# A chunked RWKV-7 scan on one Trainium2 core: the triangular inverse kept as 32x32 diagonal blocks instead of full 64x64 matrices

## The chip, the cores and the metric

The kernel runs on one core of one Trainium2 chip. The metric is the device time of one execution in microseconds (us), lower is better. Durations and waits come from one profiled execution of the kernel before.

## What is computed

The reference is a two-layer backbone over 256 latent tokens and 256 context tokens, width 1024. Each layer has three mixers (a bidirectional RWKV-7 scan, latent attention, a Fourier mix), a gated merge and a feed-forward network. The change touches the scan alone:

```python
def rwkv_scan(state0, f, d, reverse):
    ...
    def step(S, inp):
        r_t, w_t, k_t, v_t, kk_t, b_t = inp
        sa = -jnp.einsum("bhvk,bhk->bhv", S, kk_t)
        S = S * w_t[:, :, None, :] + sa[..., None] * b_t[:, :, None, :] + v_t[..., None] * k_t[:, :, None, :]
        return S, jnp.einsum("bhvk,bhk->bhv", S, r_t)
```

It has 8 heads of 64, two directions, and in each layer runs over the context first and then over the latent tokens. All of it is float32.

## The kernel before

**Chunks.** The scan takes 64 tokens at a time. Within a chunk the 64 values of `sa` depend on each other through a strictly triangular 64x64 matrix L, so `sa` comes from the inverse of I + L. Each layer has 512 tokens, which makes 8 chunk steps, and the two layers make 16. A step does both directions (d = 0 and 1) beside each other. Layer 1 needs the outputs y in all 8 steps, layer 2 in the last 4 only, so 12 steps have the work for y and 4 have not.

**Layout.** Two heads lie one above the other on the 128 partitions (`UP` is partitions 0 to 63, `DOWN` is 64 to 127), and four such pairs lie beside each other. `each` (L1250) issues 8 matmuls for one product of all heads: 4 pairs times two, each 64 rows by 64 columns, on the two diagonal 64x64 tiles of TensorE. The profile has two records for each float32 matmul, so `x16` is one such product.

**A step on TensorE (PE), in its order.** (1) For each direction the Gram products (L1281, L1282, L1287): B against Q and R into bank B_LT (128 columns), Q against B into B_L (64 columns), K against Q and R into B_G (128 columns). (2) Transposes of B and K (L1292) and of V (L1301). (3) Levels 1 to 4 of the inverse (L1303 to L1318): the inverse T is built from blocks of 2, 4, 8, 16, 32. POOL masks L into `LM` (L1060), PE multiplies LM by T (`x1`), ACT copies the product to `X1` (L1116), PE multiplies T by X1 and X1 by T (`tx`, two products), and DVE subtracts both from T and its transpose (`T2`, L1208). (4) Level 5 joins the two 32x32 halves: `halves` (L1263) does it with 8 matmuls of 32x32 for each product, and DVE subtracts (L1213). (5) W (L1329), the part of y that comes from the state (L1335), `sa` = T times W (L1341, by `each`), the part of y that comes from `sa` (L1347), and the state product (L1356). Then the next step's Gram products follow.

**What waits for what.** The engines run through semaphores, one queue each, in the order that is written. In a level PE waits for DVE (T) and POOL (LM), ACT and POOL for PE, PE again for ACT (X1), and DVE for PE. DVE has other work between the levels in its queue: `gram_out` (L1183) and `keep` (L1173) after levels 1 and 2, the next chunk's `operands` (L1164 to L1166) and `exponents` (L1152, L1153) after level 3, and `operands` again after level 5. DVE also makes level 0 (L1194 masks, L1196 adds the identity, L1200 masks ARB). ACT copies `WS` (L1133) before `sa` and SA_V (L1137) after it; both parts behind `sa` on PE wait for L1137.

## Time and profile before

| | us |
|---|---|
| median of 3 runs | 2377.68 (2368.16 to 2380.21) |
| the profiled execution, its own time | 2380.61 |
| its span, first to last instruction | 2378.8 |
| PE busy in the span | 2090.7 |
| DVE busy | 1170.2 |
| ACT busy | 832.9 |
| POOL busy | 340.1 |

The two scans lie from about 234.5 to 489.5 us and from 1589.8 to 1837.7 us of the span. A row of the timeline has the start, how long it lasted, the engine, the line, what is written and read, the number of records, and in brackets how long the engine was idle before it and what released it. The times of PE rows include the time until the last result is there. PEclk 1.00 is 2.4 GHz and 0.50 is 1.2 GHz.

### The profile page before, as it was taken

What the parts mean: (1) busy time and instruction counts of PE and PEld (TensorE: products, weight loads), DVE (VectorE), ACT (ScalarE), POOL (GpSimd) and SP (SyncE); (2) the same over time, 40 slices, a digit from 0 to 9 for tenths busy, and PEclk for the clock granted to TensorE, in tenths of its full rate; (3) what the DMA queues carried; (4) which work ended last, traced back from release to release, by engine and by line L of the source; (5) the groups of instructions that cost most, each with busy time, mean ns of one, the idle gap of its engine ahead of it and who ended that gap; (6) DMA issues with size and microseconds to landing.
All of it is one profiled execution on the core that took longest, in us unless ns stands there. A gap on an engine that the chain in (4) does not pass through costs nothing. (4 is left out here: it accounts for less than half of the span.)

```text
span 2378.8 us, 46796 instructions
## 1 busy us (share of the span) xinstructions
PE 2090.7 (88%) x19559; PEld 1651.7 (69%) x19559; DVE 1170.2 (49%) x1849; ACT 832.9 (35%) x1515; POOL 340.1 (14%) x444
## 2 busy tenths in 40 slices
PE   4886889869989999889998997968888798988998
PEld 2562788844457888658886665738887446988988
DVE  1635787762462333353332216477777435545544
ACT  1333443423342222242222113264443244434442
POOL 1102333301100011010001001043332020000000
PEclk7997999989989999989999998979999899998999
DMA  7416000030111333222235753000000311553553
GB/s 261 142 62 230 2 0 2 1 118 21 36 38 54 98 94 101 71 71 94 88 102 218 283 168 124 27 1 1 1 1 26 113 36 56 169 178 124 178 174 128
DMA packets 144521, 219.40 MB, mean 92 GB/s; under 512 B 6846, under 2 KB 123800, under 8 KB 137216
## 3 DMA queue, kind: packets, MB, share of 16 engines
q1 hardware_dynamic: 142880, 215.74, 26.7%
q8 instruction: 101, 1.65, 0.3%
q0 software_dynamic: 1504, 1.71, 0.2%
q14 instruction: 36, 0.29, 0.0%
HBM read 208.00 MB, written 9.44 MB: 91 GB/s over the span
## 5 line engine op out<-in xcount | busy, mean ns | idle before, releaser
L367 PE MATMUL BANK<-H_high,W_high 128*128 128x512 f32 (+2 forms) x1472 | 526.4, 358 | 79.5 <-ACT H_high L628 36.1
L331 DVE TENSOR_TENSOR W_low<-RING,W_high 128x1024 fp32r<-128x1024 f32 x268 | 328.2, 1234 | 459.1 <-ACT W_high L328 459.1
L368 PE MATMUL BANK<-H_low,W_high 128*128 128x512 f32 (+2 forms) x1472 | 520.3, 353 | 0.0
L369 PE MATMUL BANK<-H_high,W_low 128*128 128x512 f32 (+2 forms) x1472 | 519.7, 353 | 0.0
L328 ACT ACTIVATE W_high<-RING 128x1024 fp32r<-128x1024 f32 x268 | 279.3, 1052 | 614.8 <-PE BANK L369 597.9
L367 PEld LDWEIGHTS BANK<-H_high,W_high 128*128 128x128 f32 (+1 forms) x1472 | 283.5, 193 | 134.6 <-issue 52.1
L369 PEld LDWEIGHTS BANK<-H_high,W_low 128*128 128x128 f32 (+1 forms) x1472 | 283.9, 193 | 38.1
L368 PEld LDWEIGHTS BANK<-H_low,W_high 128*128 128x128 f32 (+1 forms) x1472 | 284.2, 193 | 36.6 <-issue 1.1
L1255 PE MATMUL BANK<-RING,WORK 64*64 64x64 f32 x4096 | 166.8, 220 | 17.2 <-DVE RING L1208 8.7
L1255 PEld LDWEIGHTS BANK<-RING,WORK 64*64 64x64 f32 x4096 | 145.4, 134 | 29.9 <-issue 29.5
L1060 POOL TENSOR_TENSOR WORK<-WORK,masks 128x256 f32<-128x256 f32 x160 | 125.3, 795 | 115.6 <-PE BANK L1255 115.0
L367 PE MATMUL BANK<-hidden_high,W_high 128*128 128x512 f32 (+1 forms) x352 | 121.8, 346 | 12.0 <-PEq L2062 12.0
L368 PE MATMUL BANK<-hidden_low,W_high 128*128 128x512 f32 (+1 forms) x352 | 119.5, 339 | 0.0
L369 PE MATMUL BANK<-hidden_high,W_low 128*128 128x512 f32 (+1 forms) x352 | 119.3, 339 | 0.0
L1255 PE MATMUL BANK<-WORK,RING 64*64 64x64 f32 x2560 | 107.8, 224 | 4.1 <-issue 1.8
L1116 ACT ACTIVATE WORK<-BANK 128x256 f32<-128x256 f32 (+1 forms) x160 | 56.5, 362 | 133.4 <-PE BANK L1255 124.5
L2000 POOL TENSOR_TENSOR merge_tiles<-merge_tiles 128x512 f32<-128x512 f32 (+1 forms) x32 | 33.8, 1067 | 480.2 <-DVE merge_tiles L1982 480.2
L1255 PEld LDWEIGHTS BANK<-WORK,RING 64*64 64x64 f32 x2560 | 93.4, 139 | 9.4 <-issue 7.7
L1208 DVE TENSOR_TENSOR RING<-RING,BANK 128x512 f32<-128x512 f32 x128 | 83.8, 683 | 31.6 <-PE BANK L1255 29.0
L1255 PE MATMUL BANK<-RING 64*64 64x128 f32 (+1 forms) x1536 | 78.3, 261 | 21.1 <-DVE RING L1166 21.1
L367 PEld LDWEIGHTS BANK<-hidden_high,W_high 128*128 128x128 f32 x352 | 67.3, 191 | 34.9 <-issue 27.7
L1255 PEld LDWEIGHTS BANK<-RING 64*64 64x64 f32 x1536 | 74.5, 139 | 23.2 <-issue 22.3
(281 smaller groups left out, 3110.9 us busy)
## 6 DMA issues: line engine op xcount, KB each, us to landing
modulation_weights<-w_mod_dram SPq DMA_DIRECT2D x48, 1024.0 KB, 6.9
RING<-w_in_dram SPq DMA_DIRECT2D x46, 1024.0 KB, 5.9
RING<-w_ffn_in_dram SPq DMA_DIRECT2D x44, 1024.0 KB, 5.1
RING<-w_ffn_out_dram SPq DMA_DIRECT2D x20, 1024.0 KB, 5.1
RING<-w_out_dram SPq DMA_DIRECT2D x8, 1024.0 KB, 5.4
h_high<-H_high SPq DMA_DIRECT2D x2, 2048.0 KB, 8.2
h_low<-H_low SPq DMA_DIRECT2D x2, 2048.0 KB, 12.5
H_high<-h_high SPq DMA_DIRECT2D x2, 2048.0 KB, 12.0
```

The lines of the kernel that those rows point to most:

```text
L328: high_ready.mark(nc.scalar.activation(self.part(0, c), self.raw(c), ACT.Copy))
L331: low_ready.mark(nc.vector.tensor_tensor(self.part(1, c), self.raw(c), self.part(0, c).bitcast(FP32), ALU.subtract))
L367: nc.tensor.matmul(out, w[0], x[0], start=start, stop=False)
L368: nc.tensor.matmul(out, w[0], x[1], start=False, stop=False)
L369: return nc.tensor.matmul(out, w[1], x[0], start=False, stop=stop)
L1060: s_lm[d].mark(nc.gpsimd.tensor_tensor(LM[d], LTS[d], lanes(level_mask(d, l)), ALU.mult))
L1116: s_x1_out[d].mark(nc.scalar.activation(X1[d][:, :, cols], pairs(4 * d + B_L, 0)[:, :, cols], ACT.Copy))
L1208: s_t[d].mark(nc.vector.tensor_tensor(T2[d].rearrange("p q j t -> p (q j t)"), T2[d].rearrange("p q j t -> p (q j t)"), BANK[:, 4 * d + B_ ...
L1255: last = nc.tensor.matmul(BANK[rows, bank, at + j * stride:at + j * stride + width], lhs(j)[rows], rhs(j)[rows], start=True, stop=True)
L2000: pool_sig.mark(nc.gpsimd.tensor_tensor(total(m), total(m), gate(u), ALU.add))
```

## The change

T2 now holds three sets of 32x32 blocks: the diagonal blocks of T, those of its transpose, and the one off-diagonal block. Levels 1 to 4 need only the diagonal blocks. `each_block` takes the place of `each` there: 16 matmuls of 32 rows by 32 columns in place of 8 of 64 by 64, on the four diagonal tiles in turn. The tiles that DVE, ACT and POOL handle in the levels become half as wide.

```diff
-    T2 = [scratch(2, PAIRS, HD) for _ in range(NDIR)]
+    T2 = [scratch(3, PAIRS, BLOCK) for _ in range(NDIR)]
...
-    LTS = [scratch(PAIRS, HD) for _ in range(NDIR)]
-    LM = [scratch(PAIRS, HD) for _ in range(NDIR)]
-    X1 = [scratch(PAIRS, HD) for _ in range(NDIR)]
+    LTS = [scratch(2, PAIRS, BLOCK) for _ in range(NDIR)]
+    LM = [scratch(PAIRS, BLOCK) for _ in range(NDIR)]
+    X1 = [scratch(PAIRS, BLOCK) for _ in range(NDIR)]
```

TensorE: the Gram products that feed the inverse are made block by block (`gram_blocks`, 64 rows by 32 columns), the levels by `each_block`, level 5 by `across` (as many matmuls as `halves`), and `sa` by two matmuls for each head, one with the diagonal block (32 rows) and one with the two blocks of the other row (64 rows):

```diff
+                def each_block(bank, at, lhs, rhs):
+
+                    for j in range(PAIRS):
+                        for b in range(P // BLOCK):
+                            rows = slice(b * BLOCK, (b + 1) * BLOCK)
+                            last = nc.tensor.matmul(BANK[rows, bank, at + j * BLOCK:at + (j + 1) * BLOCK], lhs[rows, j], rhs[rows, j],
+                                                    start=True, stop=True)
+                    return last
...
+                def gram_blocks(bank, at, lhs, rhs, wide=None):
+
+                    for j in range(PAIRS):
+                        for half in (slice(0, BLOCK), slice(BLOCK, HD)):
+                            for h, rows in enumerate((UP, DOWN)):
+                                if half == wide:
+                                    out = BANK[of_head(h, half), bank, HALF:2 * HALF].rearrange("p (b j t) -> p b j t", b=2, j=PAIRS)[:, :, j]
+                                    cols = slice(0, HD)
+                                else:
+                                    out, cols = BANK[of_head(h, half), bank, at + j * BLOCK:at + (j + 1) * BLOCK], half
+                                last = nc.tensor.matmul(out, lhs(j)[rows, half], rhs(j)[rows, cols], start=True, stop=True)
...
-                        s_gram[d].mark(each(bank + B_LT, 0, 2 * HD, lambda j: BK[d][:, j, 0], qr))
-                        s_gram[d].mark(each(bank + B_L, 0, HD, q, lambda j: BK[d][:, j, 0], 2 * HD))
+                        gram_blocks(bank + B_LT, near(d), b, q, wide=first_half(d))
+                        s_gram[d].mark(each(bank + B_LT, 0, HD, b, lambda j: QR[d][:, j, 1]))
+                        s_gram[d].mark(gram_blocks(bank + B_L, near(d), q, b))
...
-                                s_x1[d].mark(each(4 * d + B_L, 0, HD, lambda j: LM[d][:, j], lambda j: T2[d][:, 0, j]))
+                                s_x1[d].mark(each_block(4 * d + B_L, 0, LM[d], T2[d][:, 0]))
...
-                                each(4 * d + B_LT, 0, HD, lambda j: T2[d][:, 1, j], lambda j: X1[d][:, j])
-                                s_tx[d].mark(each(4 * d + B_LT, HALF, HD, lambda j: X1[d][:, j], lambda j: T2[d][:, 1, j]))
+                                each_block(4 * d + B_LT, 0, T2[d][:, 1], X1[d])
+                                s_tx[d].mark(each_block(4 * d + B_LT, BLOCKS, X1[d], T2[d][:, 1]))
...
-                        s_sa[d].mark(each(4 * d + B_LT, 0, HD, lambda j: T2[d][:, 1, j], lambda j: WS[d][:, j]))
+                        for j in range(PAIRS):
+                            for h, rows in enumerate((UP, DOWN)):
+                                one = of_head(h, first_half(d))
+                                out = slice(j * HD, (j + 1) * HD)
+                                nc.tensor.matmul(BANK[one, 4 * d + B_LT, out], T2[d][one, 1, j], WS[d][one, j], start=True, stop=True)
+                                last = nc.tensor.matmul(BANK[of_head(h, later_half(d)), 4 * d + B_LT, out], T2[d][rows, 2, j], WS[d][rows, j],
+                                                        start=True, stop=True)
+                        s_sa[d].mark(last)
```

The other engines: ACT gets one more pair of copies for each direction in level 5 and a new signal `s_later` that `sa` waits for, POOL no longer masks in level 5, and DVE writes the off-diagonal block with a copy in place of the subtraction.

```diff
-                        for d in range(NDIR):
+                        for d in range(NDIR if l < NL else 0):
...
-                            s_x1_out[d].mark(nc.scalar.activation(X1[d][:, :, cols], pairs(4 * d + B_L, 0)[:, :, cols], ACT.Copy))
+
+                            s_x1_out[d].mark(nc.scalar.activation(X1[d], blocks(4 * d + B_L, 0), ACT.Copy, scale=1.0 if l < NL else -1.0))
+                        for d in range(NDIR if l == NL else 0):
+
+                            act.wait_ge(*at_step(s_t[d], i, LEVELS, NL))
+                            act.wait_ge(*at_step(s_sa[d], i))
+                            for h in range(2):
+                                rows = of_head(h, later_half(d))
+                                last = nc.scalar.activation(T2[d][rows, 2], T2[d][rows, 1], ACT.Copy)
+                            s_later[d].mark(last)
...
-                                    last = nc.vector.tensor_tensor(T2[d][rows, 1, :, cols], T2[d][rows, 1, :, cols],
-                                                                   pairs(4 * d + B_LT, HALF)[rows, :, cols], ALU.subtract)
+                                    rows = of_head(h, first_half(d))
+                                    last = nc.vector.tensor_copy(T2[d][rows, 2], blocks(4 * d + B_LT, BLOCKS)[rows])
```

TensorE's queue at the end of a step, before. The names in these rows are those of whole memories; the last numbers are the output's partitions by its columns. L1268 is level 5, L1329 is W, L1335 the first part of y, L1255 is `sa`, L1347 the second part of y, L1356 the state product.

```order
L1268 MATMUL BANK<-RING,WORK 32x32 x32
L1329 MATMUL BANK<-WORK,RING 64x64 x16
L1335 MATMUL BANK<-RING,WORK 64x64 x16
L1339 REGISTER_ALU
L1255 MATMUL BANK<-WORK,RING 64x64 x16
L1347 MATMUL BANK<-WORK 64x64 x16
L1356 MATMUL BANK<-WORK 64x64 x16
```

The same place now. L1296 is level 5, L1373 W, L1379 the first part of y, L1390 and L1391 are `sa`; they alternate 16 times (6 of the 32 rows are shown).

```order
L1296 MATMUL BANK<-RING,WORK 32x32 x16
L1373 MATMUL BANK<-WORK,RING 64x64 x16
L1379 MATMUL BANK<-RING,WORK 64x64 x16
L1383 REGISTER_ALU
L1390 MATMUL BANK<-WORK,RING 32x64
L1391 MATMUL BANK<-WORK,RING 32x64
L1390 MATMUL BANK<-WORK,RING 32x64
L1391 MATMUL BANK<-WORK,RING 32x64
L1390 MATMUL BANK<-WORK,RING 32x64
L1391 MATMUL BANK<-WORK,RING 32x64
```

The one group of 16 matmuls of a single form became 32 matmuls, and their form changes from each one to the next.

TensorE's queue at the start of a step (the Gram products), before:

```order
L1255 MATMUL BANK<-RING 64x128 x8
L1255 MATMUL BANK<-RING 64x64 x8
L1255 MATMUL BANK<-RING 64x128 x16
L1255 MATMUL BANK<-RING 64x64 x8
L1255 MATMUL BANK<-RING 64x128 x8
L1292 MATMUL BANK<-ident,RING 128x128 x8
```

The same place now, from the end of the first direction's first product on:

```order
L1310 MATMUL BANK<-RING 32x32 x2
L1274 MATMUL BANK<-RING 64x64 x8
L1310 MATMUL BANK<-RING 32x32 x16
L1274 MATMUL BANK<-RING 64x128 x8
L1310 MATMUL BANK<-RING 32x32 x2
L1310 MATMUL BANK<-RING 32x2x32 x2
```

Each direction had 24 matmuls of one form. It now has 48, with three changes between the forms of L1310 and L1274 within it and one more to the next direction.

## Rows read from the trace of the kernel before

**Rows 1.** The page, busy time of each engine over the whole span.

```profile
PE 2090.7 (88%) x19559; PEld 1651.7 (69%) x19559; DVE 1170.2 (49%) x1849; ACT 832.9 (35%) x1515; POOL 340.1 (14%) x444
```

**Rows 2.** Busy time by stretch: stretch, its length, then each engine.

```profile
core 0: us, PE busy (x) PEld busy (x) DVE busy (x) ACT busy (x) POOL busy (x), PEclk, DMA share, GB/s
234.50:489.50 255.00, 225.86 (x5746) 207.82 (x5742) 189.75 (x328) 107.38 (x278) 91.73 (x127) 0.98 0.01 1
1589.80:1837.70 247.90, 219.27 (x5486) 201.88 (x5482) 186.72 (x320) 107.24 (x278) 91.97 (x127) 0.97 0.00 1
```

**Rows 3.** Timeline of POOL, the first row of three successive steps.

```profile
1742.00 0.18 POOL L1052 COPY decay_kept<-decay 64x8 f32<-64x8 f32 x1 [8.53 <-DVE WORK L1239]
...
1774.73 0.18 POOL L1052 COPY decay_kept<-decay 64x8 f32<-64x8 f32 x1 [10.01 <-DVE WORK L1239]
...
1805.91 0.18 POOL L1052 COPY decay_kept<-decay 64x8 f32<-64x8 f32 x1 [8.47 <-DVE WORK L1239]
```

**Rows 4.** Timeline of PE in the step from 1774 us on.

```profile
1773.82 4.64 PE L1255 MATMUL BANK<-RING 64*64 64x128 f32 x96
...
1781.49 0.68 PE L1255 MATMUL BANK<-RING,WORK 64*64 64x64 f32 x16 [0.42 <-DVE RING L1196]
...
1789.81 0.66 PE L1255 MATMUL BANK<-RING,WORK 64*64 64x64 f32 x16
1790.28 0.66 PE L1255 MATMUL BANK<-WORK,RING 64*64 64x64 f32 x16
...
1797.46 0.61 PE L1268 MATMUL BANK<-RING,WORK 32*32 32x32 f32 x32 [0.66 <-ACT WORK L1116]
1798.00 1.15 PE L1329 MATMUL BANK<-WORK,RING 128*64 128x64 f32 x32
1798.98 1.10 PE L1335 MATMUL BANK<-RING,WORK 128*64 128x64 f32 x32
1800.02 1.15 PE L1255 MATMUL BANK<-WORK,RING 64*64 64x64 f32 x32
1801.66 1.47 PE L1347 MATMUL BANK<-WORK 64*64 64x64 f32 x32 [0.49 <-ACT WORK L1137]
1803.07 2.08 PE L1356 MATMUL BANK<-WORK 128*64 128x64 f32 x32
```

**Rows 5.** Timeline of DVE, levels 1 to 4 of the same step.

```profile
1783.24 0.69 DVE L1208 TENSOR_TENSOR RING<-RING,BANK 128x512 f32<-128x512 f32 x1 [1.13 <-PE BANK L1255]
1784.08 0.69 DVE L1208 TENSOR_TENSOR RING<-RING,BANK 128x512 f32<-128x512 f32 x1
...
1787.15 1.28 DVE L1208 TENSOR_TENSOR RING<-RING,BANK 128x512 f32<-128x512 f32 x2
...
1791.00 1.29 DVE L1208 TENSOR_TENSOR RING<-RING,BANK 128x512 f32<-128x512 f32 x2
1792.20 0.42 DVE L1164 TENSOR_TENSOR RING<-WORK 128x256 f32<-128x256 f32 x1
1792.54 0.42 DVE L1165 TENSOR_TENSOR RING<-WORK 128x256 f32<-128x256 f32 x1
...
1794.95 1.27 DVE L1208 TENSOR_TENSOR RING<-RING,BANK 128x512 f32<-128x512 f32 x2
```

**Rows 6.** Groups with their forms: mean duration of one record in ns.

```profile
L1255 PE MATMUL BANK<-RING,WORK 64*64 64x64 f32 x4096 | 166.8, 220 | 17.2 <-DVE RING L1208 8.7 <-DVE RING L1196 4.9 <-issue 1.1
L1268 PE MATMUL BANK<-RING,WORK 32*32 32x32 f32 x1024 | 25.0, 193 | 19.2 <-DVE RING L1208 9.0 <-ACT WORK L1116 9.0
L1116 ACT ACTIVATE WORK<-BANK 128x256 f32<-128x256 f32 x128 | 49.0, 383 | 128.0 <-PE BANK L1255 124.5
L1116 ACT ACTIVATE WORK<-BANK 128x128 f32<-128x128 f32 x32 | 7.5, 275 | 5.4 <-PE BANK L1268 5.1
```

**Rows 7.** Timeline of ACT between level 5 and W.

```profile
1797.51 0.59 ACT L1130 ACTIVATE WORK<-BANK 64x512 f32<-64x512 f32 x1
1798.73 0.85 ACT L1133 ACTIVATE WORK<-BANK 128x256 f32<-128x256 f32 x2 [0.63 <-PE BANK L1329]
```

**Rows 8.** Busy time by stretch, around two falls of the clock (columns as in Rows 2).

```profile
1762.60:1765.90 3.30, 2.04 (x84) 1.87 (x86) 1.45 (x4) 2.69 (x9) 0.72 (x1) 1.00 0.00 0
1766.00:1769.30 3.30, 3.30 (x66) 3.18 (x62) 1.58 (x5) 0.77 (x2) 0.00 (x0) 0.50 0.00 0
...
1670.50:1673.80 3.30, 1.97 (x87) 1.70 (x83) 1.65 (x4) 2.73 (x9) 0.72 (x1) 1.00 0.00 0
1673.90:1677.20 3.30, 3.30 (x63) 3.12 (x59) 2.23 (x7) 1.05 (x4) 0.00 (x0) 0.50 0.00 0
```

More of the change, by code:

```diff
@@ L65 @@
 LEVELS = 6
+BLOCK = 32
 SLOTS = 3
@@ L125, in shape_constants @@
         level = []
-        for l in range(LEVELS):
+        for l in range(LEVELS - 1):
             b = 1 << l
@@ L133, in shape_constants @@
         parts = [-(level[0].T.astype(f)), -(level[0].astype(f))] + [m.astype(f) for m in level[1:]]
-        parts += [strict_t.astype(f), incl_t.astype(f)]
-        masks.append(np.concatenate([stack(m) for m in parts], axis=1))
+        block_masks += [np.concatenate([m[0:BLOCK, 0:BLOCK]] * (P // BLOCK), axis=0) for m in parts]
+        masks += [stack(strict_t.astype(f)), stack(incl_t.astype(f))]
     out["masks"] = np.concatenate(masks, axis=1).astype(f)
-    out["eye_heads"] = stack(np.eye(HD)).astype(f)
+    out["block_masks"] = np.concatenate(block_masks, axis=1).astype(f)
+    out["eye_blocks"] = np.concatenate([np.eye(BLOCK)] * (P // BLOCK), axis=0).astype(f)
     return out
@@ L981, in build_in @@
     NL = LEVELS - 1
+    NM = NL - 1
     N = SEG_CHUNKS
     def lanes(mask):
-        return mask.unsqueeze(1).to_broadcast([P, PAIRS, HD])
+        return mask.unsqueeze(1).to_broadcast([P, PAIRS, BLOCK])
     STEPS = 2 * N
@@ L1032, in scan @@
         pairs = lambda bank, a: BANK[:, bank, a:a + HALF].rearrange("p (j t) -> p j t", j=PAIRS)
+        BLOCKS = PAIRS * BLOCK
+        blocks = lambda bank, a: BANK[:, bank, a:a + BLOCKS].rearrange("p (j t) -> p j t", j=PAIRS)
+        near = lambda d: HALF + BLOCKS * d
         with stage() as block:
@@ L1239, in step @@
                         s_st[d].mark(nc.vector.tensor_tensor(STATE_V[d][UP], STATE_V[d][UP], SD[d][UP], ALU.add))
+                for d in range(NDIR):
+                    nc.vector.memset(BANK[:, 4 * d + B_LT, HALF:2 * HALF], 0.0)
                 nc.vector.memset(STATE_V[0][UP], 0.0)
@@ L1267, in halves @@
                             k = of_head(h, k_rows)
-                            last = nc.tensor.matmul(BANK[of_head(h, out_rows), bank, at + j * HD + out_cols.start:at + j * HD + out_cols.stop],
-                                                    lhs[k, j, out_rows], rhs[k, j, out_cols], start=True, stop=True)
+                            last = nc.tensor.matmul(BANK[of_head(h, out_rows), bank, at + j * BLOCK:at + (j + 1) * BLOCK], lhs[k, j], rhs[k, j],
+                                                    start=True, stop=True)
+                    return last
+                def gram_blocks(bank, at, lhs, rhs, wide=None):
[8 more added lines that the diff above has]
+                                last = nc.tensor.matmul(out, lhs(j)[rows, half], rhs(j)[rows, cols], start=True, stop=True)
                     return last
```

58 lines of the change are left out of this document (32 added, 26 removed).

## The prediction

> **What bounds the kernel now.** I read the busy shares first. Over the whole span PE is busy 2090.7 of 2378.8 us [rows 1], but a busy PE is not a PE at its peak, and the change touches the two scans alone. Busy time by stretch gives them 255.0 and 247.9 us, 503 us together or 21% of the span, and in both PE (89%) and DVE (75%) are busy side by side [rows 2]. So neither has much slack there. Everything else keeps its instructions, and I cost it at nothing: the new constants are one small load more behind loads that nobody in the opening waits for.
>
> POOL's first row of a step gives the pitch of the steps: 1774.73 to 1805.91, 31.2 us, and 32.7 us for the step before it [rows 3]. There are 16 steps, so 0.1 us in a step is 1.6 us of the kernel. The timeline of PE shows what a step is made of [rows 4], that of DVE who sets the pace of the levels [rows 5]: in level 1 DVE waits 1.13 us for PE, but the pairs of L1208 at 1787.15, 1791.00 and 1794.95 begin with no wait, right behind DVE's other work. In levels 2 to 4 DVE is the bound, with the round trip PE, ACT, PE close behind it.
>
> **What the change gains.** One product of a level is 16 records on two tiles, and the next begins 0.47 us after it (1789.81 to 1790.28) [rows 4]. The new product has 32 records of 32x32. The nearest row is L1268, which has 32 such records in 0.61 us [rows 4], of which 0.19 is the latency of the last [rows 6]: 0.42 us. It uses two tiles for each direction and the new product uses four at once, so 0.42 is the upper end that I use, and half of it, 0.21, the lower. I take 0.35: a gain of 0.1 us a product. The Trainium skill ("TensorE: Matmul & The Clock Gate", section "Measured speedup vs the span model") has tiles of a pack start about 4 ns apart; by it the product would be at the lower end, and the sum below some 1.5 us a step lower.
>
> The pair of L1208 works on 512 columns a direction in 1.28 us. With 256 columns the nearest rows are L1164 and L1165: 0.42 us for one and the next 0.34 us behind it, so 0.76 for a pair [rows 5]. That is 0.5 us less in each of levels 2 to 4, all of it on the path there: 1.5 us. In level 1, where PE is waited for, three products of a direction, a copy on ACT (383 to 275 ns [rows 6]) and the subtraction shrink, about 0.3 + 0.1 + 0.2 = 0.6 us. At the start of the levels L1194 and L1196 become half as wide, and PE's wait of 0.42 us for L1196 [rows 4] goes. Level 5 has as many matmuls as before. POOL's mask halves and is off the path. Together **2.5 us a step gained**. The bounds: 1.5 if the new products take as long as the old ones, 4.0 if they take 0.21.
>
> **What it costs.** The main term is a cost on PE that the old order pays only a few times a step. When the form of the matmuls (rows by columns of the tile) changes, the next one starts late. L1347 (64x64) lasts 1.47 from 1801.66; less the 0.22 of its last record, that record starts at 1802.91, and L1356 (128x64) starts at 1803.07: 0.16 us. From L1268 (32x32, last start 1797.46 + 0.61 - 0.19 = 1797.88) to L1329 (128x64) at 1798.00 it is 0.12. Between two products of one form it is 1789.81 + 0.66 - 0.22 = 1790.25 to 1790.28: 0.03 [rows 4, 6]. So a change costs 0.12 to 0.16 us from start to start, about 0.1 more than none.
>
> *sa.* It was 16 matmuls of one form, 1.15 us less 0.22, 0.93 us [rows 4]. It is now 32 matmuls that alternate between a 32x32 tile (L1390) and a 64x32 tile (L1391), 32 changes. Each matmul is two records on one tile; their distance is about 0.05 us (16 records of 64x64 on two tiles in 0.47 us are 0.058 apart on one tile, with somewhat wider weights [rows 4]). 0.05 + 0.13 = 0.18 us a matmul, 5.8 us in place of 0.93: **4.9 us a step**. The lower bound is 0.15 (3.9 us), the upper 0.22 (6.1 us). It lies on the path: y and the state product are queued behind it on PE, L1137 on ACT waits for it, and the next step's Gram products follow. One piece comes back: PE waited 0.49 us for L1137 [rows 4], and the first direction's L1137 is now hidden behind the second direction's `sa`. I take back 0.4: 4.5 us.
>
> *Gram products.* The 96 records were 4.64 us [rows 4]. There are now 8 changes of form in them at 0.1, 0.8 us, and the narrower streams give back some 0.4 (the 128-column product of L becomes blocks of 64 and 32 columns). Cost **0.4 us**, between 0 and 1.
>
> *ACT.* Four copies of 32x128, at most 0.28 each by the 128x128 copy [rows 6], come between L1116 and L1130. ACT was idle 0.63 us before L1133 [rows 7], and `sa` began 0.44 us after L1133 was done (1799.58 to 1800.02). These two cover the 0.8 to 1.1 us, so nothing; if that cover is gone (the 4 steps without y), up to 0.4 us each, under 2 us in all.
>
> Without the clock, a step costs 4.5 + 0.4 - 2.5 = 2.4 us more, 16 steps 38 us.
>
> **The clock.** In the scans PE's granted clock is 0.98 and 0.97 on the mean [rows 2]. It falls to 0.50 (1.2 GHz) now and then, each time behind the stretch with level 5, where PE had run 32x32 matmuls with waits between them: 1762.6 to 1765.9 had PE busy 2.04 of 3.30 us, and 1766.0 to 1769.3 ran at 0.50; 1670.5 to 1673.8 and 1673.9 to 1677.2 are the same [rows 8]. The step with the first of these falls is the one that took 32.7 us in place of 31.2 [rows 3]: 1.5 us a fall. After the change all the levels run on 32x32 matmuls, and `sa` is 5.8 us in which the array mostly waits. I expect two more such stretches in each step: **3.0 us a step**, 48 us in all. Nothing excludes none, nor four.
>
> **The sum.** 2380.6 (the profiled execution) + 38 + 48 = 2467 us. That execution lies 3 us above the median of the runs, so the forecast is **2464 us**, slower by 3.6%.
>
> **The rivals.**
> 1. *The forms' changes cost what I say and the clock holds.* For it: after `sa` the Gram products are as dense as before. Against it: [rows 8]. 2377.7 + 38 = 2416 us.
> 2. *Faster.* The place is `sa`: if PE does not wait between a 32x32 and a 64x32 matmul, it is 32 matmuls of 0.05 us spread over tiles, about 1 us as now, and the clock then falls about as rarely as now. 2.5 - 0.4 = 2.1 us a step gained, 34 us: 2344 us. It decides where a change costs less than 0.1 - 2.4/32 = about 0.03 us. For it: the trace of before has no such pair of forms. Against it: both kinds of change above, one of rows alone and one of rows and columns, cost 0.12 us or more from start to start. The Trainium skill ("TensorEngine Tiling (Array Packing)", section "Key Properties") says that each change of the tiling mode drains the engine, which leaves this rival little.
> 3. *The levels themselves get slower.* If a 32x32 record cannot come faster than a 64x64 one does, 0.029 us, a product of 32 records takes 0.93 us in place of 0.47. That is 24 products by 0.47, 11 us a step; about two thirds of it show, since PE then bounds the levels: 7 us more and the gain of 1.0 on PE gone, 2464 + 16 x 8 = 2590 us. Against it: L1268 has its 32 records in 0.42 us, 0.013 each. The Trainium skill ("TensorEngine Tiling (Array Packing)", section "Instruction Overhead") has about 60 cycles for each matmul however few its columns are, and warns against cutting a dimension that is small already; that speaks against this change, and the row speaks against the rule.
>
> **How the numbers follow.** My forecast has a chance of 0.55 (its own range 2416 to 2530: the bounds of `sa`, of the levels and of one to four stretches of low clock), rival 1 has 0.25, rival 2 has 0.12, rival 3 has 0.05, and 0.03 is left for no real difference (gain and cost cancel). About 0.5% is what a measurement of this kernel can tell from no change. The range that leaves out rival 2 and rival 3 and keeps the low side of rival 1 is 2380 to 2535. Slower by over 0.5% are my forecast, rival 1 and rival 3, 0.85 together, less 0.02 for the low end of rival 1: 0.83. Faster by over 0.5% is rival 2: 0.12. The same is what is left: 0.05.
>
> **What would show it.** Right: in the timeline L1390 and L1391 as alternating rows about 0.18 us apart, some 5.8 us from the first to the last; L1227 (the old L1208) at about 0.42 us; the products of L1287 at most 0.42 us apart; a mean clock in the scans of 0.7 to 0.9. Wrong: `sa` under 2 us; products of L1287 over 0.5 us apart; a clock that stays at 0.97; or a step shorter than 31 us.

## The result and the profile after

The changed kernel takes **2740.5 us** (median of 4 runs, 2739.19 to 2745.27) against 2376.3 for the kernel before beside it: ratio 1.1538, 95% interval 1.152 to 1.1556. It is slower, as forecast, but by 364 us and not by 86, and above the range. All of it lies in the two scans. In the profiled execution (span 2738.9 us, mean clock 0.835, before 0.943) they end near 670 and 2200 us, where they ended at 489.5 and 1837.7 [rows 2].

Of the page, the busy time of PE, the fetches of program code (queue q8), and the groups of the levels with their idle time, as in [rows 1] and [rows 6]:

```profile
PE 2323.6 (85%) x27751; PEld 1784.7 (65%) x27751; DVE 1093.5 (40%) x1853; ACT 840.2 (31%) x1579; POOL 274.7 (10%) x412
...
q8 instruction: 242, 3.96, 0.6%
...
L1287 PE MATMUL BANK<-RING,WORK 32*32 32x32 f32 x8192 | 158.8, 224 | 93.7 <-issue 90.5
...
L1227 DVE TENSOR_TENSOR RING<-RING,BANK 128x256 f32<-128x256 f32 x128 | 53.9, 421 | 223.6 <-PE BANK L1287 223.2
...
L1287 PE MATMUL BANK<-WORK,RING 32*32 32x32 f32 x4096 | 85.5, 225 | 48.5 <-issue 43.5
```

DVE's merge is as short as forecast (421 ns), and DVE now waits for PE. But PE's products of the levels have 134 us of idle time ahead of them that ends on nothing but "issue", where the old products had 2.9 (L1255, groups of 4096 and 2560). And q8 fetched 242 pieces of code; the page of before has 101. The lines of before, beside the one in [rows 6]:

```profile
q8 instruction: 101, 1.65, 0.3%
...
L1255 PE MATMUL BANK<-WORK,RING 64*64 64x64 f32 x2560 | 107.8, 224 | 4.1 <-issue 1.8
```

Busy time by stretch, as in [rows 2]: the clock in the scans is 0.62 and 0.61, not 0.98 and 0.97.

```profile
234.50:670.00 435.50, 339.97 (x9693) 272.46 (x9684) 151.37 (x328) 109.84 (x308) 56.27 (x105) 0.62 0.02 4
1760.00:2200.00 440.00, 340.83 (x9615) 267.53 (x9608) 154.48 (x339) 112.41 (x313) 60.56 (x112) 0.61 0.03 7
```

POOL's first row of three steps, as in [rows 3]: 54.8 and 58.6 us, in place of 31 to 33.

```profile
1968.81 0.18 POOL L1061 COPY decay_kept<-decay 64x8 f32<-64x8 f32 x1 [20.51 <-DVE WORK L1256]
...
2023.58 0.18 POOL L1061 COPY decay_kept<-decay 64x8 f32<-64x8 f32 x1 [24.22 <-DVE WORK L1256]
...
2082.16 0.18 POOL L1061 COPY decay_kept<-decay 64x8 f32<-64x8 f32 x1 [24.22 <-DVE WORK L1256]
```

The timeline of PE in the levels of the step behind the third of these rows shows both sides of the change, as in [rows 4]:

```profile
2095.72 0.75 PE L1287 MATMUL BANK<-RING,WORK 32*32 32x32 f32 x64
2096.67 0.42 PE L1287 MATMUL BANK<-WORK,RING 32*32 32x32 f32 x29 [0.20 <-ACT WORK L1126]
...
2096.95 0.40 PE L1287 MATMUL BANK<-RING,WORK 32*32 32x32 f32 x23
2099.51 0.26 PE L1287 MATMUL BANK<-RING,WORK 32*32 32x32 f32 x8 [2.16 <-issue]
...
2099.93 1.70 PE L1287 MATMUL BANK<-RING,WORK 32*32 32x32 f32 x84
2103.19 0.42 PE L1287 MATMUL BANK<-RING,WORK 32*32 32x32 f32 x11 [1.56 <-issue]
...
2104.72 0.54 PE L1287 MATMUL BANK<-RING,WORK 32*32 32x32 f32 x20
2107.34 0.43 PE L1287 MATMUL BANK<-RING,WORK 32*32 32x32 f32 x12 [2.08 <-issue]
```

A product of 32 records begins 0.28 us behind the start of the one before it (2096.67 to 2096.95), so records come 0.009 us apart. Then, in the middle of a product, PE stands for 2.16 us. The pauses end 3.7 and 4.2 us apart, and between them lie about 128 records, 64 matmuls. The pause of 2.16 us lies where the granted clock is 1.00 (2094 to 2100 us), so a lowered clock is not its cause. The DMA view of one step points at the reason: 12 pieces of code in 58.6 us, of 0.20 MB / 12 = 16 KB each. In the same view of two steps of before (1742 to 1806 us), no packet is moved.

```profile
GB/s 0 11 0 0 11 0 0 0 11 0 0 11 0 0 11 0 0 11 0 11 0 0 11 0 0 11 0 0 11 0 0 0 0 0 0 0 0 0 11 11
DMA packets 12, 0.20 MB, mean 3 GB/s; under 512 B 0, under 2 KB 0, under 8 KB 0
...
q8 instruction: 12, 0.20, 1.4%
```

The same view of 2096 to 2108 us, in slices of 0.3 us, has its three pieces at 2097, 2100.6 and 2104.5 us. Each is fetched some 2.4 to 2.8 us before a pause ends, and the next only some 1.3 us after PE has begun again. So the distance of 3.7 to 4.2 us is that of about 64 matmuls and the way of one piece. Whether pieces could come closer together if they were asked for sooner, no run shows.

The second part of the loss is `sa`. Its alternating rows are 0.35 us apart and not 0.18, and the whole takes 2065.26 to 2076.35, 11.1 us. The row by stretch over it says where a part of this comes from: granted clock 0.50, 1.2 GHz.

```profile
2065.26 0.42 PE L1390 MATMUL BANK<-WORK,RING 32*32 32x64 f32 x2
2065.60 0.42 PE L1391 MATMUL BANK<-WORK,RING 64*32 64x64 f32 x2
2065.95 0.41 PE L1390 MATMUL BANK<-WORK,RING 32*32 32x64 f32 x2
...
2076.35 2.14 PE L1399 MATMUL BANK<-WORK 64*64 64x64 f32 x32
...
2065.26:2076.70 11.44, 11.44 (x72) 5.97 (x72) 0.00 (x0) 1.00 (x3) 0.00 (x0) 0.50 0.01 1
```

### The profile page after: what moved, and what is told of

Same layout as the page of the kernel before. It is cut to its first block and busy times, and to the rows that moved or that the text cites. A ratio compares the mean times of both kernels' runs of the same rounds, so it can differ in the third digit from the quotient of the medians.

```text
span 2738.9 us, 63339 instructions
## 1 busy us (share of the span) xinstructions
PE 2323.6 (85%) x27751; PEld 1784.7 (65%) x27751; DVE 1093.5 (40%) x1853; ACT 840.2 (31%) x1579; POOL 274.7 (10%) x412
## 5 line engine op out<-in xcount | busy, mean ns | idle before, releaser
L1287 PE MATMUL BANK<-RING,WORK 32*32 32x32 f32 x8192 | 158.8, 224 | 93.7 <-issue 90.5
L1287 PEld LDWEIGHTS BANK<-RING,WORK 32*32 32x32 f32 x8192 | 133.0, 136 | 105.0 <-issue 103.4
L1227 DVE TENSOR_TENSOR RING<-RING,BANK 128x256 f32<-128x256 f32 x128 | 53.9, 421 | 223.6 <-PE BANK L1287 223.2
L1126 ACT ACTIVATE WORK<-BANK 128x128 f32<-128x128 f32 x160 | 44.3, 277 | 276.4 <-PE BANK L1287 226.3
L1287 PE MATMUL BANK<-WORK,RING 32*32 32x32 f32 x4096 | 85.5, 225 | 48.5 <-issue 43.5
L1287 PEld LDWEIGHTS BANK<-WORK,RING 32*32 32x32 f32 x4096 | 70.0, 137 | 64.3 <-issue 63.0
L1391 PE MATMUL BANK<-WORK,RING 64*32 64x64 f32 x512 | 101.2, 296 | 0.0
L1390 PE MATMUL BANK<-WORK,RING 32*32 32x64 f32 x512 | 99.9, 292 | 0.0
L1310 PE MATMUL BANK<-RING 64*32 64x32 f32 (+1 forms) x2048 | 46.4, 230 | 43.6 <-issue 22.5
```

The lines of the kernel that those rows point to most:

```text
L1126: s_x1_out[d].mark(nc.scalar.activation(X1[d], blocks(4 * d + B_L, 0), ACT.Copy, scale=1.0 if l < NL else -1.0))
L1227: s_t[d].mark(nc.vector.tensor_tensor(both, both, BANK[:, 4 * d + B_LT, 0:HALF], ALU.subtract))
L1287: last = nc.tensor.matmul(BANK[rows, bank, at + j * BLOCK:at + (j + 1) * BLOCK], lhs[rows, j], rhs[rows, j], start=True, stop=True)
L1310: last = nc.tensor.matmul(out, lhs(j)[rows, half], rhs(j)[rows, cols], start=True, stop=True)
L1390: nc.tensor.matmul(BANK[one, 4 * d + B_LT, out], T2[d][one, 1, j], WS[d][one, j], start=True, stop=True)
L1391: last = nc.tensor.matmul(BANK[of_head(h, later_half(d)), 4 * d + B_LT, out], T2[d][rows, 2, j], WS[d][rows, j], start=True, stop=True)
```

## The experiments

My theory after the result: the 364 us are (a) code that no longer stays loaded in PE, with pauses wherever the small matmuls run densely, (b) the order of forms in `sa`, and (c) a clock that falls behind both. The rivals: the pauses belong to the small matmuls themselves, or to the clock, or to the jump back of the loop.

Most of the kernels below ran once. The runs of the kernel before lie between 2368 and 2380 us, so a difference of under some 12 us between two single runs is not shown by these alone.

**sa_grouped.** The 32x32 matmuls of `sa` of a direction first, then the 64x32 ones: 4 changes of form a step instead of 32.

```diff
                         for j in range(PAIRS):
-                            for h, rows in enumerate((UP, DOWN)):
+                            for h in range(2):
...
                                 nc.tensor.matmul(BANK[one, 4 * d + B_LT, out], T2[d][one, 1, j], WS[d][one, j], start=True, stop=True)
+                        for j in range(PAIRS):
+                            for h, rows in enumerate((UP, DOWN)):
+                                out = slice(j * HD, (j + 1) * HD)
                                 last = nc.tensor.matmul(BANK[of_head(h, later_half(d)), 4 * d + B_LT, out], T2[d][rows, 2, j], WS[d][rows, j],
                                                         start=True, stop=True)
```

> The changed kernel with the 16 matmuls of sa in each direction sorted by form: 8 of 32x32, then 8 of 64x32, so 4 changes of form a step in place of 32. Theory (each change of form waits until the array is empty, and sa's 11.1 us a step are that): sa falls to about 2 to 3 us, the kernel by 16 x 8.5 = 136 us or more, to about 2600. Rival (the new forms themselves are slow, 0.35 us a matmul whatever stands beside them): no difference, 2740.

Measured 2618.6 us, 122 less. Order alone is worth a third of the loss. The steps are still 41.5 to 51.3 us, and the pauses are still there: PE has 135.4 us of idle time on "issue" ahead of the products of the levels.

**before_unrolled.** The kernel before, with the loop over steps written out on every engine.

```diff
-                Signal.trips = end - first
-                with eng.Fori(first, end) as i:
+                Signal.trips = 1
+                for i in range(first, end):
```

> The kernel before with the scan's loops written out, so that no code is used twice; the work is the same. Theory (the pauses of about 2 us on TensorE in the changed kernel come from 16 KB pieces of code that are fetched at a rate that only dense short matmuls outrun): code is fetched in all steps, about 6 pieces a step, and the time stays within 1% of before, with at most a few pauses. Rival (each fetch of code costs a pause of 2 us wherever it is): 14 steps x 6 x 2 = 168 us slower, about 2545.

Measured 2380.3 us, no difference. This execution fetched 157 pieces, 12 of them from 1742 to 1806 us, and its clock in the first scan is 0.98. The two groups of L1255 have 3.6 us of idle time on "issue", as little as before. So fetching code is not a cost in itself: a step of before spends 64 matmuls in 31.2 x 64 / 368 = 5.4 us, more than the 3.7 to 4.2 us between two pieces in the changed kernel.

**y_interleaved and y_in_turn.** The kernel before with 28 more changes of form (64x64 and 128x64) in each step with y, and its control with the same matmuls in turn.

```diff
                         order = [(k, one) for one in heads() for k in range(2)]
+                        order = [x for x in order if x[0] == 0] + [x for x in order if x[0] == 1]
```

(The line with + stands in y_in_turn alone.)

> As y_in_turn, but with the 8 matmuls of y (64x64) and the 8 of the state product (128x64) of a direction in turn: 31 changes of form in a step with y in place of 3, the number of matmuls unchanged. Theory (a change costs 0.12 to 0.16 us from start to start at 2.4 GHz, up to 0.24 at 1.2 GHz): 28 x 0.1 to 0.2 x 12 steps = 34 to 67 us over y_in_turn, about 2425. Rival (a change of form between other forms is free, and only 32-row against 64-row tiles wait): no difference from y_in_turn.

> The kernel before with the second part of y and the state product of one direction behind each other, then the other direction; in a step with y that is 3 changes of form in place of 1. It is the control for y_interleaved. Both theories: within 1% of before, perhaps 0.5% slower (2 changes x 0.12 us x 12 steps = 3 us).

Measured 2481.5 and 2379.2 us: 102 us for 12 x 28 = 336 changes, 0.30 us each with the clock. I had expected 34 to 67 us: the mechanism held, and my price for a change was too low by half or more. The timeline of y_interleaved has a matmul of two records each 0.25 us at the full clock and each 0.40 us at half:

```profile
1844.19 0.33 PE L1355 MATMUL BANK<-WORK 128*64 128x64 f32 x2
1844.45 0.32 PE L1350 MATMUL BANK<-WORK 64*64 64x64 f32 x2
1844.70 0.33 PE L1355 MATMUL BANK<-WORK 128*64 128x64 f32 x2
...
1810.13 0.47 PE L1350 MATMUL BANK<-WORK 64*64 64x64 f32 x2
1810.54 0.47 PE L1355 MATMUL BANK<-WORK 128*64 128x64 f32 x2
```

So a pair of forms with no 32-row tile in it costs this too, and the rival that only 32-row against 64-row tiles wait is out.

**levels_looped.** PE's levels 1 to 4 as a loop of four turns inside the step: the same matmuls run, but PE's body has 336 matmuls in the code and not 624. The transposes of V of direction 1 move behind level 4, and ACT's copy of them to level 5.

```diff
+                    turn_values(0)
+                    if True:
+                        Signal.trips *= NL - 1
+                        with pe.Fori(1, NL) as l:
+                            level(l)
+                        Signal.trips //= NL - 1
...
+                    turn_values(1)
+                    level(NL, True)
```

> The changed kernel with TensorE's levels 1 to 4 of a step as a loop of its own of four turns, so that its products stand once in the code and not four times: the same matmuls run, TensorE's loop body shrinks from about 2,500 instructions (624 matmuls of 4) to about 1,350 (336). The transposes of the values of direction 1 move behind level 4. Theory (the pauses of 1.5 to 2.2 us on no wait, some 12 us a step, are TensorE waiting for its own code, because the body no longer stays loaded): the code fetches inside the loop and the pauses go, 16 steps x 12 us = 190 us less: 2,550 us. Rival 1 (the pauses belong to the small matmuls or to the lowered clock, not to code): they stay, 2,740 us. Rival 2 (each jump back costs a pause of about 2 us as the one behind the step's own jump, 4 more a step): 2,550 + 16 x 8 = 2,680 us, with the pauses at the levels' ends instead of inside the groups.

**levels_written_out.** The control: the same placement, with `for l in range(1, NL)` in place of the loop.

> The control for levels_looped: the same placement of the transposes of the values of direction 1 behind level 4, with the levels written out as in the changed kernel, so that TensorE's loop body has about 2,500 instructions again. Theory (code): the pauses are back, 2,720 to 2,760 us. Rival (moving the transposes gave part of the 219 us): below 2,700 us.

Measured **2521.3 us** with the loop and **2761.6 us** without: 240 us by nothing but how often the code stands in the program. q8 has 97 pieces in place of 242, and the steps are 38 to 39 us, but for the first turn of each loop (42 to 45 us). Of the page of levels_looped, the larger group of the levels: its idle time was 93.7 us, 90.5 of it on "issue", and DVE ends most of what is left.

```profile
L1287 PE MATMUL BANK<-RING,WORK 32*32 32x32 f32 x8192 | 120.6, 202 | 34.7 <-DVE RING L1227 24.3
```

The rival that the small matmuls pause by themselves is out, and so is a pause for every jump back. The control is 21 us slower than the changed kernel: with the transposes moved, the idle time on "issue" ahead of the products of the levels is 154.6 us in place of 134.

**levels_looped_grouped.** Both edits.

> As levels_looped, and with the sa product's 32 matmuls ordered by form (8 of 32x32, then 8 of 64x32, for each direction). If code and changes of form are separate costs, the 122 us that ordering alone gave come off as well: 2,550 - 122 = 2,430 us. If what ordering gave was mostly fewer pauses or a clock that follows from them, less comes off: 2,500 us or more. A time below 2,376 us would mean that the idea of the change was sound and only its code order was not.

Measured 2393.4 us: 128 less, as much as ordering gave with the pauses there. The two costs add. The steps are now 30 to 31 us, but the first turn of each loop takes 35 to 36. PE's timeline of such a turn, and the busy time by stretch around it:

```profile
1719.62 0.86 PE L1287 MATMUL BANK<-RING,WORK 32*32 32x32 f32 x64
...
1724.12 0.28 PE L1287 MATMUL BANK<-WORK,RING 32*32 32x32 f32 x10 [2.52 <-issue]
...
1712.00:1722.00 10.00, 9.11 (x362) 7.72 (x360) 6.16 (x12) 4.15 (x9) 4.38 (x8) 1.00 0.02 5
1722.00:1732.00 10.00, 6.62 (x427) 6.07 (x427) 6.45 (x13) 2.35 (x9) 2.54 (x5) 0.68 0.01 2
```

One pause for code of 2.5 us, and the clock falls behind it: this is how (a) can bring (c). No run takes the clock by itself.

**after_short and before_short.** Levels 2 to 4 with one pair of heads in four, in the changed kernel and in the one before.

```diff
-                    for j in range(PAIRS):
+                    for j in range(n):
...
-                                s_x1[d].mark(each_block(4 * d + B_L, 0, LM[d], T2[d][:, 0]))
+                                s_x1[d].mark(each_block(4 * d + B_L, 0, LM[d], T2[d][:, 0], PAIRS if l < 2 else 1))
...
```

> The changed kernel with levels 2, 3 and 4 of the inverse left out for three of the four pairs of heads (the result is not the inverse then; 216 of 624 matmuls a step go), in straight code: the loop body has about 1,700 instructions without any inner loop. Theory (code): no fetches inside the loop and no pauses on no wait over 1 us; steps of 30 to 36 us, 2,390 us. Rival (the pauses come from dense small matmuls): pauses of 2 us stay in level 1 and beside it, at least 4 us a step, and the steps are 40 us, 2,500 us.

> The control for after_short: the kernel before, with levels 2, 3 and 4 left out for three of the four pairs in the same way (108 of 368 matmuls a step). Its levels are bounded by the chain through four engines, so that little goes: steps of 27 to 29 us against 31, 2,310 to 2,350 us. What after_short is above it is the price of the sa product's and the Gram products' changes of form, with the clock, without code pauses: 32 changes x 0.25 to 0.35 us a step as a bound would be 8 to 11 us x 16 = 130 to 180 us; less what the levels gain.

Measured 2579.6 and 2397.3 us; both expectations missed. A body of 408 matmuls (some 1,690 instructions) was not short enough everywhere. The two loops of the first scan have the same body, and yet one fetched 8 or 9 pieces in every turn and the other none. Busy time by stretch of a turn of the first and one of the second, and the DMA view of the first:

```profile
320.60:368.00 47.40, 37.59 (x800) 29.34 (x800) 18.80 (x42) 13.97 (x40) 7.53 (x14) 0.64 0.01 3
459.10:500.00 40.90, 34.80 (x803) 26.57 (x802) 18.66 (x43) 14.04 (x40) 7.53 (x14) 0.67 0.00 0
```

```profile
q8 instruction: 9, 0.15, 1.3%
```

The same 800 records take 47.4 us with fetches and 40.9 without. So the steps of 30 to 36 us that I expected were not reached without fetches either: the rest of the miss is the order of `sa` and the clock, 0.67 in that turn. Why the one loop kept its code and the other did not (where it lies in the program is what differs) was not tried.

before_short does less than the kernel before and is 19 us slower (one run). Its clock is what differs: 0.79 in the first scan, where the full kernel has 0.98 [rows 2].

```profile
234.50:489.50 255.00, 196.48 (x3836) 174.03 (x3833) 183.31 (x320) 104.49 (x271) 88.18 (x122) 0.79 0.00 1
```

PE has less to do between the waits for the same chain, and the clock falls more often. That the one brings the other is my reading.

**after_unrolled.** The changed kernel with the loops over steps written out: no jump back.

> The changed kernel with its two loops of a scan written out on every engine: 8 steps in a row, no jump back, every piece of code is used once. If the pauses come from the rate at which pieces of code arrive (one for 64 matmuls), they stay and the time is that of the changed kernel within 1%: 2,720 to 2,770 us. If they come from the jump back, which throws loaded code away, they go: 2,560 us or less.

Measured 2693.3 us, 47 less than with the loops and below what I expected of the rate alone. In the changed kernel the first product behind a jump back (L1310) has 22.5 us of idle time on "issue"; here that is gone, so the jump back has a part, some 47 us with what follows from it. But most of the cost of code stays when every piece is used once. The groups of the levels have 130 us on "issue", as against 134:

```profile
L1287 PE MATMUL BANK<-RING,WORK 32*32 32x32 f32 x8192 | 155.9, 225 | 90.3 <-issue 85.8
...
L1287 PE MATMUL BANK<-WORK,RING 32*32 32x32 f32 x4096 | 85.5, 226 | 49.0 <-issue 44.3
```

**gram_one_loop.** levels_looped_grouped with the 64x32 products of a direction ahead of its 64x64 ones, and the first scan in one loop of 7 steps.

```diff
+                        s_gram[d].mark(gram_blocks(bank + B_L, near(d), q, b))
                         gram_blocks(bank + B_LT, near(d), b, q, wide=first_half(d))
                         s_gram[d].mark(each(bank + B_LT, 0, HD, b, lambda j: QR[d][:, j, 1]))
-                        s_gram[d].mark(gram_blocks(bank + B_L, near(d), q, b))
```

> levels_looped_grouped, and two more edits of order: of the Gram products of each direction the 64x32 ones (L and its transpose) come first and the 64x64 ones behind, which takes 2 changes of form for a direction and 4 for a step away; and the first scan, whose two halves have the same step, runs as one loop of 7 steps, so that its first turn's extra time (35.5 against 30 us, a code pause of 2.5 us and the lowered clock behind it) is paid once, not twice. 4 x 0.145 us x 16 = 9 us and 5 us: 2393 - 14 = 2,379 us. If Gram is hidden behind another engine: 2,388 us.

Measured 2384.6 us, 9 less, which two single runs do not show by themselves. The timelines do: from the first Gram product to the transposes behind them it is 5.18 us in levels_looped_grouped (1778.04 to 1783.22) and 4.68 with the new order (side_work_spread, 1793.45 to 1798.13), both at a clock of 1.00. That is 0.5 us a step, 8 us in all: a small term.

**split_merge.** DVE's merge as two operations, the first behind the first product.

```diff
-                                s_t[d].mark(nc.vector.tensor_tensor(both, both, BANK[:, 4 * d + B_LT, 0:HALF], ALU.subtract))
+                                s_ta[d].mark(nc.vector.tensor_tensor(one[0], one[0], BANK[:, 4 * d + B_L, BLOCKS:2 * BLOCKS], ALU.subtract))
+                                dve.wait_ge(*at_step(s_tx[d], i, NL, l))
+                                s_t[d].mark(nc.vector.tensor_tensor(one[1], one[1], BANK[:, 4 * d + B_LT, BLOCKS:2 * BLOCKS], ALU.subtract))
...
```

> gram_one_loop, and VectorE's merge of T and its transpose in levels 1 to 4 as two operations of half the columns instead of one, the first of which starts behind the first of the two products (which goes to another bank for that). The next level's first product needs T alone. If the wait of 0.68 us on VectorE's merge ahead of each level's first product is what bounds a level, it shrinks by the second product (0.21 us) and by half of the merge (0.42 to 0.25 us), about 0.4 us x 4 levels x 16 steps = 25 us: 2,355 us, below the kernel before. Rival (the wait moves on to the merge of the transpose, or to ScalarE's copy): 2,380 us as gram_one_loop.

**side_work_spread and spread_split_merge.** DVE's masking of the Gram products of direction 1 goes behind level 4, both copies of q and r behind level 2; the second also has the split merge.

```diff
-                        if l <= NDIR:
-                            gram_out(l - 1)
-                            keep(i, l - 1)
+                        if l in (1, 4):
+                            gram_out(l // 4)
+                        if l == 2:
+                            keep(i, 0)
+                            keep(i, 1)
```

> gram_one_loop (2,384.6 us), with VectorE's work between the merges placed otherwise: the masking of the Gram products of direction 1 behind level 4 instead of level 2, the copies of q and r of direction 0 behind level 2 instead of level 1. In split_merge VectorE's merge started only when 2.4 us of such work behind levels 1 and 2 was done. If that holds the levels here too: up to 0.3 us x 2 levels x 16 = 10 us less: 2,375 us. If a level is bound by the chain x1, copy, products, merge: 2,385 us.

> side_work_spread with the merge split in two (as in split_merge, 2,379.6 us). With VectorE free when the first product is done, a level ends 0.3 to 0.4 us sooner: 4 levels x 0.35 x 16 = 22 us: 2,355 us. If the levels are bound by the chain through ScalarE's copy and the wait before the second products: 2,375 us.

Measured 2379.6, 2373.7 and 2385.7 us. Spreading DVE's work came out 11 us lower, but the steady steps with y are alike (30.8 us in gram_one_loop, 30.7 here), so it is not shown that the spreading did it. Splitting the merge came out 5 lower without it and 12 higher with it, no more than single runs differ. None of the 22 to 25 us that I expected of it came: that the wait for the merge bounds a level to the amount I took was wrong.

**before_looped.** The control: the kernel before with PE's level loop, the one loop in the first scan and DVE's side work spread in the same way.

> The kernel before with the edits of form that the better variants of the changed kernel have: TensorE's levels 1 to 4 as a loop of four turns, one loop of 7 steps in the first scan, VectorE's side work at other levels (as in side_work_spread). Its code stayed loaded anyway and its levels are bounded by VectorE's merges of 1.1 us, so that nothing is to be gained but the first turns' 1.8 us: 2,365 to 2,385 us. Should it be much faster, the forms' gain is not the change's.

**before_looped_timed and side_work_spread_timed.** Both again, in turns with the kernel before.

> before_looped again, timed in turns with the kernel before: one look gave 2,362.96 against 2,375.79 us. If the edits of form alone make the kernel before faster, the ratio is 0.993 to 0.997 with an interval below 1; if one look misled, it holds 1.

> side_work_spread again, timed in turns with the kernel before: one look gave 2,373.68 against 2,375.79 us: ratio 0.997 to 1.001. Against before_looped_timed it says what the 32x32 blocks are worth once the code stays loaded and the forms are in order: one look says 11 us slower.

before_looped takes 2363.0 us in the first run and 2363.2 in 6 more, ratio 0.9951 (0.9938 to 0.9963). side_work_spread takes 2374.2 in 12 more, ratio 0.9994 (0.9984 to 1.0004). So with code and forms in order the 32x32 blocks still lost 11 us against a control of the same shape. Its timeline has PE idle ahead of W's second direction (L1390), and at half clock behind it; ACT's timeline has what W waits for, the copy of V (L1143), queued behind the four copies of the later blocks (L1133):

```profile
1782.96 0.69 PE L1390 MATMUL BANK<-WORK,RING 128*64 128x64 f32 x16
1784.57 1.12 PE L1390 MATMUL BANK<-WORK,RING 128*64 128x64 f32 x16 [0.92 <-issue]
...
1785.00:1788.00 3.00, 3.00 (x62) 2.88 (x58) 0.32 (x1) 0.77 (x2) 0.00 (x0) 0.53 0.00 0
```

```profile
1782.47 1.28 ACT L1133 ACTIVATE RING<-RING 32x128 f32<-32x128 f32 x4
1783.77 0.59 ACT L1143 ACTIVATE WORK<-BANK 64x512 f32<-64x512 f32 x1
```

**values_earlier.** side_work_spread with that copy ahead of the four, and the copy of direction 1's doubled values (L1148) behind the copies of W.

```diff
+                        if l == NL:
+                            d = 1
+                            act.wait_ge(*at_step(s_v_turned[d], i, 1, 1))
+                            act.wait_ge(*at_step(s_ds[d], i))
+                            s_v_tok[d].mark(nc.scalar.activation(STATE_V[d][DOWN].rearrange("p g t -> p (g t)"), BANK[DOWN, 4 * d + B_S], ACT.Copy))
                         for d in range(NDIR if l == NL else 0):
...
+                    act.wait_ge(*at_step(s_v_tok[1], i, 1, 1))
+                    s_sa_v[1].mark(nc.scalar.activation(SA_V[1][DOWN].rearrange("p g t -> p (g t)"), BANK[DOWN, 4 + B_S], ACT.Copy))
```

> side_work_spread (ratio 0.9994) with ScalarE's copy of direction 1's values ahead of the four copies of the inverse's later blocks (1.28 us), and the copy of the doubled values behind the copies of W. TensorE stood 0.92 us on no named wait ahead of W's second direction, which needs that copy; in before_looped, which has no copies of later blocks, W's 32 matmuls run through. The prediction took these copies as covered. If they are what W waits for: 0.9 us x 16 = 14 us less, 2,360 us, ratio 0.993 to 0.996, level with before_looped (0.9951): then the blocks themselves are worth nothing either way. If the wait only moves behind W: 2,374 us.

Measured **2340.9 us** in 5 runs, ratio **0.9849** (0.983 to 0.9868): 1.5% faster than the kernel before, faster than before_looped too, and more than twice the gain that I expected of it. W's 32 records run through, and then the clock does not fall in this step: a step in steady state takes 28.2 us at 1.00, where side_work_spread took 30.7 at 0.94. (The first turn of a loop still takes 31 to 34 us, so that the whole gains less than 16 times that.) The two moves of copies were made together, and which of them gave how much is not shown. before_looped did not get them, but it had no such wait to lose: there W, the first part of y and `sa` follow each other without idle time on PE.

```profile
1745.98 0.74 PE L1297 MATMUL BANK<-RING,WORK 32*32 32x32 f32 x64 [0.56 <-DVE RING L1235]
...
1748.85 0.74 PE L1297 MATMUL BANK<-RING,WORK 32*32 32x32 f32 x64 [0.58 <-DVE RING L1235]
...
1756.67 1.15 PE L1397 MATMUL BANK<-WORK,RING 128*64 128x64 f32 x32
...
1758.74 0.64 PE L1414 MATMUL BANK<-WORK,RING 32*32 32x64 f32 x16
...
1761.00 0.68 PE L1426 MATMUL BANK<-WORK 64*64 64x64 f32 x16
...
1737.35:1765.50 28.15, 23.95 (x1235) 21.41 (x1234) 19.83 (x43) 14.02 (x40) 7.75 (x14) 1.00 0.00 0
```

## Why the prediction was wrong

The direction and two of the mechanisms were right; the size was not. Step by step:

- **"Without the clock, a step costs 4.5 + 0.4 - 2.5 = 2.4 us more."** This step failed: the sum has no term for the number of PE's instructions. I counted the change's instructions by the time that they take on the array, and never by how many there are. ("Everything else keeps its instructions" was said of what lies outside the scans, and held there: from the first product behind the second scan to the end it is 541 us before and 545 now.) PE's body grew from 368 to 624 matmuls, and at four records each (two of PE, two of PEld) from some 1,500 to some 2,550 instructions. It stopped staying loaded. The price is 219 us by levels_looped (240 against its control), 14 to 15 us a step, with the clock that falls behind the pauses. No rival had it. Rival 3 had the right sign, that the levels themselves get slower, and the highest price (2590 us, 150 short), but by another mechanism: it asked whether records can come faster than 0.029 us, and they do, every 0.009 us. That speed is what outruns the supply of code: 64 matmuls run in 128 x 0.009 = 1.2 us, and a piece for them arrives every 3.7 to 4.2. My sign of being wrong, products of L1287 over 0.5 us apart, came by the pauses between them; without a pause they are 0.28 apart, inside my 0.21 to 0.42.
- The Trainium skill ("Runtime: NRT & Kernel Launch", section "Instruction fetch mechanics") gives TensorE room for 2,048 instructions, refilled in blocks of 16 KiB or 256 instructions. That agrees with pieces of 16 KB for 64 matmuls, and with bodies of 1,500 that stay and 2,550 that don't. It does not explain the body of 1,690, which should have room and was fetched again in one of two loops. It also says that crossing a block is mostly hidden. Here the trace decides: hidden in before_unrolled, pauses of up to 2.4 us in the changed kernel (87 of them ahead of L1287, 134 us).
- **The sign.** It was not luck alone. With the code loaded (levels_looped, 2521.3 us) the loss is still 145 us, most of it by the two terms that I had, forms and clock; the rest is a wait for W that I had put in and the pauses that are left. But the forecast had 86 for them, and once `sa` and ACT's copies were in order the kernel was faster. So the sign hung on the order of 32 matmuls and a few copies, not on the blocks.
- **"0.05 + 0.13 = 0.18 us a matmul" in `sa`.** The mechanism was right, the size was not. At the full clock a matmul of two records on one tile, with its change of form, is about 0.22 us, my upper bound (in levels_looped the rows are 0.22 to 0.23 us apart); at 1.2 GHz it is 0.347, and I had priced `sa` at the full clock although I forecast that the clock falls in just this place. It was 11.1 us a step, not 5.8. With its clock, order alone cost 122 and 128 us in two pairs of runs, 8 us a step.
- **The clock, 48 us.** I expected 0.7 to 0.9 in the scans and it was 0.61 and 0.62. Its share cannot be taken apart from the other two, since it follows them. But the reason that I gave, that "all the levels run on 32x32 matmuls", is not shown: values_earlier runs the same small matmuls at 1.00 through a whole step. In the runs the clock falls behind idle stretches of 0.9 to 2.5 us (W's wait, a pause for code) and in alternating forms (in levels_looped `sa` runs at 0.22 us a matmul and then, with no wait between, at 0.35); the waits of 0.56 to 0.84 us between the levels of values_earlier did not bring it down.
- **The gain, 2.5 us a step.** Right once the code stays loaded, and if anything too small; the changed kernel itself does not show it. In values_earlier a level is 1748.85 - 1745.98 = 2.87 us, where the pairs of L1208 were 3.85 apart [rows 5]; its steady step is 2.85 us shorter than that of before_looped (31.0 at clock 1.00), although from the start of `sa` to the next product it is 2.3 us (1758.74 to 1761.00), where it was 1.6 (1800.02 to 1801.66 [rows 4]).
- **Gram products, 0.4 us a step.** Right in size: 5.18 us in levels_looped_grouped against 4.58 before (1805.07 to 1809.65), 0.6 more.
- **ACT's copies, 0.** In the changed kernel W is not held by them (L1373 runs its 32 records through). In the looped form, where I had moved V's copy behind them, the order of the copies cost 33 us (2374.2 against 2340.9).
- **"In levels 2 to 4 DVE is the bound."** So it is before the change. Behind it DVE's merge waits for PE (223 us of idle time ahead of L1227), and I had no term for PE as the bound. In values_earlier PE waits for the merge again, 0.56 to 0.84 us a level.

## What to carry to other kernels

Before cutting matmuls into smaller tiles inside a loop, count the instructions of the loop's body, not only their time: a float32 matmul is four (64 of them fill one piece of code here), and a body that no longer stays loaded turns dense small matmuls into pauses. Put what repeats into an inner loop, and order small matmuls by form; here these two edits took off 347 of the 364 us. And follow an idle stretch of PE of about a microsecond or more to what is queued ahead of its releaser, since it can cost the clock behind it too.

## What the runs showed of the hardware that I had not expected

- Code arrives in pieces of 16 KB, 64 float32 matmuls. PE paused up to 2.4 us for one where 32x32 matmuls ran 0.009 us a record, and lost nothing to be seen at 5.4 us for 64 matmuls (before_unrolled).
- The same loop body of some 1,690 instructions stayed loaded in one place of the program and not in another: 40.9 and 47.4 us a turn.
- Less work on PE can take longer: before_short, with 108 of 368 matmuls a step left out, took 19 us more than the full kernel (one run), with a clock of 0.79 in place of 0.98 in the first scan.
- With one wait of 0.92 us a steady step took 2.5 us longer: 0.92 of idle time, and 3 us behind it at 0.53 of the clock.
